# Moving eleven evictions per mixer from VectorE to ScalarE in a two-block transformer kernel

## The chip, the cores and the metric

The kernel is one program on one core of a Trainium2 chip. The metric is device time in microseconds (us) for one execution. Time is also split by engine: TensorE (PE, with its weight loads as PEld), VectorE (DVE), ScalarE (ACT), GpSimd (POOL) and the queue of SyncE (SP) that issues most transfers. TensorE's clock is granted at one of two levels, 1.2 and 2.4 GHz; a granted clock of 0.50 in a row is the lower one.

## The reference, cut to what matters

512 tokens of width 1024, fp32. A first block (sliding-window attention beside a state-space mixer, then a product-key expert layer) is followed by a second block of two layers. Each layer is a swiglu, a mixer of four parts that share one input projection, and another swiglu. The change lies in the mixers of these two layers:

```python
z = rmsnorm(x, mix_norm) @ w_in
# a: sparse attention, 4 heads of 64, the 256 best keys of an indexer
q = rmsnorm(q, g_q); k = rmsnorm(k, g_k)
logits = einsum(q, k_selected) * 64**-0.5 + bias          # softmax, times v
# b: gated linear attention, chunked
k_dec = k * exp(b_last - b);  S = exp(b_last) * S + k_dec.T @ v
# c: conv, rmsnorm, silu
# d: latent attention, 4 heads of 96
q  = (rmsnorm(c_q,  g_qa)  @ w_uq ).reshape(L, 4, 96)
kv = (rmsnorm(c_kv, g_kva) @ w_ukv).reshape(L, 4, 64 + 64)
k_nope, v = kv[..., :64], kv[..., 64:]
k = rmsnorm(concat(k_nope, k_pe), g_k)                     # then rope on 32 of the 96
y = concat([y_a, y_b, y_c, y_d]) @ w_out
```

## The kernel before, in words

Every engine's instruction stream is written out by hand. A mixer (class `Mixer`, made once for each layer) has a generator for each engine and each part: `pe_a`, `ac_a`, `ve_a` for the sparse attention, `pe_d`, `ac_d`, `ve_d` for the latent attention, `pe_b`, `ac_b`, `ve_b` for the linear attention, `*_conv` for the convolution, `ve_search` for the selection of keys. `order2` makes one list of steps, and `merged2` walks it on each engine, so the list fixes the order of each engine's queue. It begins a0 d0 c20 a1 d1 c21 a2 d2 a3 d3 a4 d4 a5 d5 a6 d6 b0 b1 a7 d7 b2 b3 a8 d8. Each engine issues in order; waits are on semaphores, and `merged2` starts on ScalarE only when every engine has ended the stage ahead of it, VectorE's last search step there being the last to end.

What the steps do, tokens in four tiles of 128:

- a0 to a3: TensorE turns (`pe_turn`, line 458) the sparse attention's queries and keys into four PSUM tiles `aT` of 128x512 (two pairs of heads, n=0 queries, n=1 keys), in banks 0 to 2. VectorE scales each by a column of gains into `qTa` (line 3419) and `kTa` (line 3421).
- d0, d1: TensorE expands the queries (line 3435), ScalarE scales them by the token's reciprocal norm (line 3478) and squares them (line 3479). d2, d3: TensorE expands keys and values (line 3442) in PSUM banks 4 to 6, and VectorE scales both halves of each of the four tiles, keys into `KD` (line 3525) and values into `VD` (line 3526).
- c21: VectorE normalizes the convolution (line 3171), ScalarE applies Silu (line 3132).
- a4: TensorE makes the first scores (lines 2687 and 2690), VectorE their maxima (lines 2761 and 2762), ScalarE their exponentials (line 2728).
- d4: ScalarE squares `KD` (line 3486); VectorE sums the squares (line 3905). d5: VectorE applies the norms (line 3914). d6, d7: VectorE does the rotary part of queries, then keys (lines 3542 to 3547).
- b0: VectorE multiplies the decayed keys (line 3680), TensorE turns them into PSUM tile `kdT` (bank 7), and VectorE copies it to `KDD` (line 3682). b1: VectorE makes a difference of decays (line 3686), ScalarE its exponential (line 3614). b2: VectorE multiplies the queries into `QX` (line 3693); TensorE's b2 and b3 wait for it (line 3570). `KDD` is read by TensorE much later, with the second block of the linear attention.

Of the kernel before, what the change touches and what calls it, by code (L numbers as in the profile page):

```python
# [13 lines left out]
ALU = mybir.AluOpType  # L14
# [708 lines left out]
class Bias:  # L723
# [23 lines left out]
    ve = po = sp = pe  # L747
# [2034 lines left out]
class Mixer:  # L2782
# [610 lines left out]
    def pe_a(self):  # L3393
        k, pe, at, l = self.k, self.k.pe, self.k.at, self.l
        for hp in range(2):
            for n, src in enumerate((self.AQ, self.AK)):
                pe.wait_ge(*at("hn", l, n))
                pe_turn(k, [src[:, i, 128 * hp:128 * hp + 128] for i in range(4)], 128, ("aT", l, hp, n), 0, 3)
                yield
        for h in range(4):  # L3400
            pe.wait_ge(*at("bt", l, h))
        yield from self.att_a.pe("aTd", l, 1, 1)

    def ac_a(self):
        k, ac, at, l = self.k, self.k.ac, self.k.at, self.l
        for _ in range(4):
            yield
        ac.wait_ge(*at("cn", l, 1))
        ac.wait_ge(*at("uqd", l, 3))
        yield from self.att_a.ac()  # L3410

    def ve_a(self):
        k, ve, v, at, l = self.k, self.k.ve, self.k.ve.e, self.k.at, self.l
        ve.wait_ge(*at("rl", l, 3, 7))
        for hp in range(2):
            for n, (g, dst) in enumerate(((f"aq{l}", self.qTa), (f"ak{l}", self.kTa))):
                ve.wait_ge(*at("aT", l, hp, n))
                if n == 0:
                    last = v.tensor_scalar(dst[:, hp, :], k.got("aT", l, hp, n), k.col(g), 0.125, ALU.mult, ALU.mult)
                else:  # L3420
                    last = v.tensor_scalar(dst[:, hp, :], k.got("aT", l, hp, n), k.col(g), None, ALU.mult)
                last.then_inc(*ve.free(("aT", l, hp, n)))
                ve.note("aTd", l, hp, n)
                yield
        yield from self.att_a.ve()

    def pe_d(self):
# [40 lines left out]
    def ac_d(self):  # L3468
        k, ac, at, l = self.k, self.k.ac, self.k.at, self.l
        a = ac.e.activation  # L3470
        for i in range(4):
            if i == 2:
                yield
            r = self.RR[:, i:i + 1]
            ac.wait_ge(*at("uqd", l, i))
            ac.wait_ge(*at("drstd", l))
            o = k.got("uq", l, i)[:, 0:384]
            a(self.QD[:, i].rearrange("p h e -> p (h e)"), o, ACT.Copy, scale=r).then_inc(*ac.up("qd", l, i))
            a(self.QSQ[:, 384 * i:384 * i + 384], o, ACT.Square, scale=r).then_inc(*ac.free(("uq", l, i)))
            ac.note("dhsq", l, i)  # L3480
        yield
        yield
        yield
        ac.wait_ge(*at("kd", l, 3))
        ac.wait_ge(*at("kdp", l))
        a(self.KSQ, self.KD.rearrange("p i h e -> p (i h e)"), ACT.Square).then_inc(*ac.up("dksq", l))
        for n in range(2):
            ac.wait_ge(*at("dhv", l, n))
            a(k.st[:, 32 + 16 * n:48 + 16 * n], k.st[:, 32 + 16 * n:48 + 16 * n],
              ACT.Sqrt).then_inc(*ac.up("dhs", l, n))  # L3490
        yield
        for _ in range(2):
            yield
        ac.wait_ge(*at("dscale", l))
        sc = k.st[:, 100:102]
        for n, dst in enumerate((self.qTd, self.kTd)):
            for h in range(4):
                ac.wait_ge(*at("dT", l, h, n))
                a(dst[0:96, h, :], k.got("dT", l, h, n)[0:96], ACT.Copy,
                  scale=sc[0:96, n:n + 1]).then_inc(*ac.free(("dT", l, h, n)))  # L3500
                ac.note("dTd", l, h, n)
                if h % 2:
                    yield

        ac.wait_ge(*at("cn", l, 1))
        yield from self.att_d.ac()

    def ve_d(self):
        k, ve, v, at, l = self.k, self.k.ve, self.k.ve.e, self.k.at, self.l
        QD, KD = self.QD, self.KD  # L3510

        sc = k.st[:, 100:102]
        v.memset(sc, 1.0).then_inc(*ve.up())
        ve.after().tensor_copy(sc[0:64, 0:1], k.col(f"dqc{l}")[0:64])
        v.tensor_copy(sc[0:64, 1:2], k.col(f"dkc{l}")[0:64]).then_inc(*ve.up())
        ve.after().tensor_scalar(sc[:, 0:1], sc[:, 0:1], 96.0 ** -0.5, None, ALU.mult).then_inc(*ve.up("dscale", l))
        yield
        yield
        for i in range(4):
            if i == 2:  # L3520
                yield
            r = self.RR[:, 4 + i:5 + i]
            ve.wait_ge(*at("ukvd", l, i))
            o = k.got("ukv", l, i).rearrange("p (h e) -> p h e", e=128)
            v.tensor_scalar(KD[:, i, :, 0:64], o[:, :, 0:64], r, None, ALU.mult)
            v.tensor_scalar(self.VD[:, i], o[:, :, 64:128], r, None, ALU.mult).then_inc(*ve.free(("ukv", l, i)))
            ve.note("kd", l, i)
        yield
        ve.wait_ge(*at("dhsq", l, 3))
        for n, (x, sq) in enumerate(((self.QSQ, ("dhsq", l, 3)), (self.KSQ, ("dksq", l)))):  # L3530
            ve_headvar(k, x.rearrange("p (i h e) -> p i h e", h=4, e=96), 4, 96, 32 + 16 * n, sq, ("dhv", l, n))
        yield
        for n, x in enumerate((QD, KD)):
            ve_headscale(k, x, 4, 96, 32 + 16 * n, ("dhs", l, n))
        yield
        R1, R2, R3, R4 = self.RT

        def rope(n, x):
            C1, S2, C2, S1 = (bc(g, 2, 4) for g in self.GT[n])
            x1, x2 = x[:, :, :, 64:80], x[:, :, :, 80:96]  # L3540
            ve.wait_ge(*at("gt", l))
            ve.after().tensor_tensor(R1, x1, C1, ALU.mult)
            v.tensor_tensor(R2, x2, S2, ALU.mult)
            v.tensor_tensor(R3, x2, C2, ALU.mult)
            v.tensor_tensor(R4, x1, S1, ALU.mult).then_inc(*ve.up())
            ve.after().tensor_tensor(x1, R1, R2, ALU.subtract)
            v.tensor_tensor(x2, R3, R4, ALU.add).then_inc(*ve.up("rope", l, n))

        rope(0, QD)
        yield  # L3550
        rope(1, KD)
        for _ in range(4):
            yield

        yield from self.att_d.ve()
# [45 lines left out]
    def ac_b(self):  # L3601
        k, ac, at, l = self.k, self.k.ac, self.k.at, self.l
        a = ac.e.activation
        CB, CS = self.CB, self.CS
        ac.wait_ge(*at("cs", l))
        for i in range(4):
            s = slice(128 * i, 128 * i + 128)
            a(self.KDT[:, s], CB[:, s], ACT.Exp, scale=-1.0, bias=CB[:, 128 * i + 127:128 * i + 128])
            last = a(self.DE[:, i:i + 1], CB[:, 128 * i + 127:128 * i + 128], ACT.Exp)
        last.then_inc(*ac.up("kde", l))  # L3610
        yield
        QES = self.ATT[0].rearrange("p h n -> p (h n)")
        ac.wait_ge(*at("qes", l))
        a(QES, QES, ACT.Exp).then_inc(*ac.up("qese", l))
        yield
        ac.wait_ge(*at("qx", l))
        a(QES, CB, ACT.Exp).then_inc(*ac.up("qe0", l))
        yield

        def block(i):  # L3620
            for n in range(10):
                if n < 8:
                    c, N = 8 * i + n, 16 * (n + 1)
                    if c >= 4:
                        ac.wait_ge(*at("ba", l, c - 4))
                    a(self.KE[c % 4][:, 0:N], CB[:, 128 * i:128 * i + N], ACT.Exp, scale=-1.0,
                      bias=CS[:, c:c + 1]).then_inc(*ac.up("kex", l, c))
                yield
            yield

        yield from block(0)
        for i in range(4):
            if i < 3:
                yield from block(i + 1)
            yield
            ac.wait_ge(*at("bo_", l, i))
            a(self.btmp[:, i], self.BV[:, i, :].rearrange("p (h e) -> p h e", e=64),
              ACT.Square).then_inc(*ac.up("bsq", l, i))
        ac.wait_ge(*at("bhv", l))
        a(k.st[:, 0:16], k.st[:, 0:16], ACT.Sqrt).then_inc(*ac.up("bhs", l))  # L3640
# [32 lines left out]
    def ve_b(self):  # L3673
# [4 lines left out]
        ve.wait_ge(*at("kde", l))  # L3678
        ve.wait_ge(*at("pj", ("bk", l)))
        v.tensor_tensor(KDT, KDT, BK, ALU.mult).then_inc(*ve.up("kdt", l))  # L3680
        ve.wait_ge(*at("kdT", l))
        v.tensor_copy(self.KDD.rearrange("p i n -> p (i n)"), k.got("kdT", l)).then_inc(*ve.free(("kdT", l)))
        ve.note("kdd", l)
        yield
        QES, QX = self.ATT[0].rearrange("p h n -> p (h n)"), self.QX
        v.tensor_tensor(QES.rearrange("p (n m) -> p n m", m=16), CB.rearrange("p (n m) -> p n m", m=16),
# [392 lines left out]
```

## Time and profile before

| | us |
|---|---|
| runs of the kernel before | 3853.77, 3854.79, 3840.77; median 3853.77 |
| profiled execution, its own time | 3855.75 |
| its span in the profile | 3854.5 |
| second stage of the first mixer, ScalarE's first instruction to the output projection | 2153.35 to 2300.84 |
| the same in the second mixer | 3294.31 to 3434.50 |

The span is what the profiled instructions cover, and the run's own time is 1.25 us longer. The two stages of the table have the same instructions; they last 147.49 and 140.19 us. A row of the timeline gives start, duration, engine, line, operation, output and inputs, and in brackets how long the engine had been idle and what ended that.

### The profile page before, as it was taken

To read this page: it belongs to the slowest core of one execution; us is meant where nothing else is said; L and a number is where in the kernel's file an instruction comes from. 1 tells how busy PE (TensorE), PEld (TensorE's weight loads), DVE (VectorE), ACT (ScalarE), POOL (GpSimd) and SP (SyncE) were. 2 spreads that over 40 slices of the span, in tenths; PEclk is the share of its full clock that TensorE was granted. 3 is DMA by queue.
4 is the path that set the end of the run, shared out by engine and by line. 5 is a ranking of instruction groups with operands and counts; after the bars stand their busy time and mean duration, and the time that the engine had idled before them with its cause. 6 is when DMAs were issued, how large, how long until landed. Compare 5 with 4: busy or idle time off the path is not lost.

```text
span 3854.5 us, 46791 instructions
## 1 busy us (share of the span) xinstructions
PE 3670.0 (95%) x18466; PEld 3098.8 (80%) x18466; DVE 2293.3 (59%) x3998; ACT 1366.0 (35%) x2368; POOL 575.0 (15%) x610
## 2 busy tenths in 40 slices
PE   9779999999999999999999689999999999689999
PEld 7767999988888888888877568888888877468887
DVE  5746899988788898433268744332433269644332
ACT  3344333444333343423243343232323243344221
POOL 8600012211445563000000100000000000100000
PEclk9779999999999999999999699999999999799999
DMA  3003388899999999233322002233223221012332
GB/s 129 12 12 93 103 276 276 269 323 331 380 375 392 388 384 360 89 94 98 104 72 60 20 23 87 95 97 104 82 94 103 88 72 55 20 50 82 99 104 72
DMA packets 275994, 574.72 MB, mean 149 GB/s; under 512 B 19952, under 2 KB 159376, under 8 KB 275648
## 3 DMA queue, kind: packets, MB, share of 16 engines
q1 hardware_dynamic: 238816, 437.42, 34.2%
q0 software_dynamic: 36864, 134.23, 9.3%
q8 instruction: 146, 2.39, 0.3%
q14 instruction: 72, 0.59, 0.0%
q10 hardware_dynamic: 96, 0.08, 0.0%
HBM read 517.92 MB, written 53.74 MB: 148 GB/s over the span
## 4 chain that ended last, share of the span: by engine, by line
PE 82%; DVE 6%; DMA 1%; ACT 1%; issue 1%; POOL 0%; DVEq 0%; SPq 0%; ACTq 0%; POOLq 0%
PE ps L358 25%; PE ps L359 24%; PE ps L360 24%; PE ps L2053 1%; PE ps L2687 1%; PE ps L590 1%; PE ps L2690 1%; PE ps L2715 1%; DVE arena L3248 1%; DVE st L3246 1%; DMA wraw<-in_ut 1%; PE ps L2697 0%; DVE arena L3149 0%; PE ps L3187 0%; PE ps L2041 0%
## 5 line engine op out<-in xcount | busy, mean ns | idle before, releaser
L349 DVE TENSOR_TENSOR wlast<-wraw,wlast 128x1024 fp32r<-128x1024 f32 x406 | 495.5, 1224 | 461.2 <-ACT wlast L339 461.1
L358 PE MATMUL ps<-XH,wlast 128*128 128x512 f32 (+2 forms) x1936 | 727.3, 376 | 18.2 <-DVE XL L637 12.5
L359 PE MATMUL ps<-XL,wlast 128*128 128x512 f32 (+2 forms) x1936 | 712.8, 368 | 0.0
L360 PE MATMUL ps<-XH,wlast 128*128 128x512 f32 (+2 forms) x1936 | 712.5, 368 | 0.0
L339 ACT ACTIVATE wlast<-wraw 128x1024 fp32r<-128x1024 f32 x406 | 426.7, 1055 | 305.4 <-PE ps L360 248.6
L349 DVE TENSOR_TENSOR wtwo<-wraw,wtwo 128x1024 fp32r<-128x1024 f32 x212 | 259.5, 1226 | 288.9 <-ACT wtwo L339 288.6
L358 PEld LDWEIGHTS ps<-XH,wlast 128*128 128x128 f32 x1936 | 368.6, 190 | 70.7 <-issue 19.8
L359 PEld LDWEIGHTS ps<-XL,wlast 128*128 128x128 f32 x1936 | 369.3, 191 | 44.5
L360 PEld LDWEIGHTS ps<-XH,wlast 128*128 128x128 f32 x1936 | 368.5, 190 | 45.3
L358 PE MATMUL ps<-XH,wtwo 128*128 128x512 f32 (+1 forms) x968 | 367.0, 379 | 2.4 <-DVE XL L637 2.4
L359 PE MATMUL ps<-XL,wtwo 128*128 128x512 f32 (+1 forms) x968 | 360.3, 372 | 0.0
L360 PE MATMUL ps<-XH,wtwo 128*128 128x512 f32 (+1 forms) x968 | 359.8, 372 | 0.0
L339 ACT ACTIVATE wtwo<-wraw 128x1024 fp32r<-128x1024 f32 x212 | 223.6, 1055 | 210.3 <-PE ps L360 163.0
L2138 POOL DMA_INDIRECT arena<-in_v,arena x128 | 237.7, 1857 | 191.8 <-DVE X L2262 86.5
L2138 POOL DMA_INDIRECT arena<-in_u,arena x128 | 148.1, 1157 | 587.6 <-DVE arena L2239 433.0
L3212 POOL TENSOR_SCALAR_AFFINE_SELECT arena<-arena 128x128 f32<-128x128 f32 x6 | 3.5, 576 | 1497.9 <-DVE arena L3232 1497.9
L358 PEld LDWEIGHTS ps<-XH,wtwo 128*128 128x128 f32 x968 | 184.9, 191 | 27.3 <-issue 2.6
L359 PEld LDWEIGHTS ps<-XL,wtwo 128*128 128x128 f32 x968 | 185.4, 192 | 24.4
L360 PEld LDWEIGHTS ps<-XH,wtwo 128*128 128x128 f32 x968 | 185.0, 191 | 24.7
L358 PE MATMUL ps<-wlast,AH 128*128 128x512 f32 x504 | 196.1, 389 | 0.0
L359 PE MATMUL ps<-wlast,AH 128*128 128x512 f32 x504 | 196.1, 389 | 0.0
L360 PE MATMUL ps<-wlast,AL 128*128 128x512 f32 x504 | 196.1, 389 | 0.0
(500 smaller groups left out, 6614.6 us busy)
## 6 DMA issues: line engine op xcount, KB each, us to landing
wraw<-in_ut SPq DMA_DIRECT2D x128, 512.0 KB, 5.2
wraw<-in_v SPq DMA_DIRECT2D x128, 512.0 KB, 7.1
wraw<-in_ffn_gate SPq DMA_DIRECT2D x88, 512.0 KB, 3.5
wraw<-in_ffn_up SPq DMA_DIRECT2D x88, 512.0 KB, 3.5
wraw<-in_ffn_down SPq DMA_DIRECT2D x88, 512.0 KB, 3.5
wraw<-in_w_in SPq DMA_DIRECT2D x58, 512.0 KB, 3.8
acts<-arena SPq DMA_DIRECT2D x128, 192.0 KB, 5.6
gates<-arena SPq DMA_DIRECT2D x12, 2048.0 KB, 12.7
```

The lines of the kernel that those rows point to most:

```text
L339: ac.e.activation(W.items[n][7], W.rawof(n), ACT.Copy).then_inc(*ac.up("whi", n))
L349: ve.e.tensor_tensor(W.items[n][8], W.rawof(n), W.items[n][7], ALU.subtract).then_inc(*ve.up("wlo", n))
L358: mm(out, lh, rh, start=start, stop=False)
L359: mm(out, lh, rl, start=False, stop=False)
L360: return mm(out, ll, rh, start=False, stop=stop)
L590: pe.e.matmul(o[:, c:c + 128], k.X[:, i, j * 128:(j + 1) * 128], self.D[i], start=True, stop=True).then_inc(*pe.up("xT", n, i, "column", j))
L2053: last = pe.e.matmul(self.gate_bank[:, 128 * (t % 4):128 * (t % 4) + 128], self.O[n % self.AHEAD][:, 0, t // 2, :, t % 2], self.RH[n % sel ...
L2138: g.indirect_dma_start(out=self.RB[n % self.ROWS], out_offset=None, in_=tables[n // PICKS], in_offset=bass.IndirectOffsetOnAxis(ap=self.PL ...
L2687: pe.e.matmul(o[:, 0:nk], self.qf(2 * hp + h, i), self.kf(2 * hp + h, nk), start=True, stop=False)
L2690: last = pe.e.matmul(o[:, lo:nk], one, x, start=False, stop=x is adds[-1][1])
L2715: last = pe.e.matmul(o[:, 64 * h:64 * h + 64], self.PT[h][:, 128 * kb:128 * kb + 128], self.V4[:, kb, 2 * hp + h, :], start=kb == 0, stop= ...
L3246: ve.after().max(m8, src).then_inc(*ve.up())
```

## The change

In each of the two mixers, ScalarE takes over three kinds of work from VectorE: the two scaled copies of turned keys (`kTa`), the eight scaled copies of the expanded keys and values (`KD`, `VD`), and the copy of the turned decayed keys (`KDD`). They become ACTIVATE instructions with function Copy; the first ten have a column as scale. On ScalarE the `kTa` copies stand in steps a1 and a3, the `KD` and `VD` copies in d2 and d3, and the `KDD` copy in b1, ahead of the exponential of line 3614. TensorE waits for one more event ahead of the first scores, since `qTa` and `kTa` now come from two engines.

```diff
@@ pe_a
+        pe.wait_ge(*at("aTd", l, 1, 0))
         yield from self.att_a.pe("aTd", l, 1, 1)
@@ ac_a
-        for _ in range(4):
+        ac.wait_ge(*at("sc", l, 3, 7))
+        for hp in range(2):
+            yield
+            ac.wait_ge(*at("aT", l, hp, 1))
+            ac.e.activation(self.kTa[:, hp, :], k.got("aT", l, hp, 1), ACT.Copy,
+                            scale=k.col(f"ak{l}")).then_inc(*ac.free(("aT", l, hp, 1)))
+            ac.note("aTd", l, hp, 1)
             yield
@@ ve_a
-            for n, (g, dst) in enumerate(((f"aq{l}", self.qTa), (f"ak{l}", self.kTa))):
...
+            ve.wait_ge(*at("aT", l, hp, 0))
+            v.tensor_scalar(self.qTa[:, hp, :], k.got("aT", l, hp, 0), k.col(f"aq{l}"), 0.125, ALU.mult,
+                            ALU.mult).then_inc(*ve.free(("aT", l, hp, 0)))
+            ve.note("aTd", l, hp, 0)
+            yield
+            yield
@@ ac_d (and the same loop, with tensor_scalar, taken out of ve_d)
+        for i in range(4):
+            if i == 2:
+                yield
+            r = self.RR[:, 4 + i:5 + i]
+            ac.wait_ge(*at("ukvd", l, i))
+            o = k.got("ukv", l, i).rearrange("p (h e) -> p h e", e=128)
+            a(self.KD[:, i, :, 0:64], o[:, :, 0:64], ACT.Copy, scale=r)
+            a(self.VD[:, i], o[:, :, 64:128], ACT.Copy, scale=r).then_inc(*ac.free(("ukv", l, i)))
+            ac.note("kd", l, i)
@@ ac_b, ahead of the wait for "qes"
+        ac.wait_ge(*at("kdT", l))
+        a(self.KDD.rearrange("p i n -> p (i n)"), k.got("kdT", l), ACT.Copy).then_inc(*ac.free(("kdT", l)))
+        ac.note("kdd", l)
@@ ve_b
-        ve.wait_ge(*at("kdT", l))
-        v.tensor_copy(self.KDD.rearrange("p i n -> p (i n)"), k.got("kdT", l)).then_inc(*ve.free(("kdT", l)))
-        ve.note("kdd", l)
```

## Rows read from the trace of the kernel before

**Rows 1.** The page: span, busy time, share and instructions of each engine

```profile
span 3854.5 us, 46791 instructions
PE 3670.0 (95%) x18466; PEld 3098.8 (80%) x18466; DVE 2293.3 (59%) x3998; ACT 1366.0 (35%) x2368; POOL 575.0 (15%) x610
```

**Rows 2.** Chain that ended last, first mixer: start, us, engine, output, line

```profile
2163.22 0.54 ACT arena L2728 x3
2163.76 1.38 ACT arena L3486
2165.16 1.76 DVE st L3905
...
2174.88 1.13 PE ps L458 x4
...
2179.57 0.59 DVE wlent L3693
```

**Rows 3.** Timeline of ScalarE, first mixer

```profile
2153.35 0.58 ACT L3478 ACTIVATE wlent<-ps,st 128x384 f32<-128x384 f32 x1 [16.33 <-DVE arena L3248]
...
2156.61 0.62 ACT L3479 ACTIVATE arena<-ps,st 128x384 f32<-128x384 f32 x1
2157.25 1.28 ACT L3132 ACT_TABLE_LOAD   x1
...
2159.71 1.28 ACT L2728 ACT_TABLE_LOAD   x1
2162.95 0.37 ACT L2728 ACTIVATE arena<-ps,st 128x128 f32<-128x128 f32 x1 [1.96 <-DVE st L2762]
...
2178.05 1.25 ACT L3499 ACTIVATE arena<-ps,st 96x512 f32<-96x512 f32 x2
```

**Rows 4.** Timeline of TensorE and VectorE, first mixer

```profile
2157.42 0.48 DVE L3525 TENSOR_SCALAR wlent<-ps,st 128x256 f32<-128x256 f32 x1
...
2158.51 1.88 PE L3442 MATMUL ps<-arena 128*128 128x512 f32 x4
...
2159.07 0.74 DVE L3421 TENSOR_SCALAR arena<-ps,cols 128x512 f32<-128x512 f32 x1
...
2160.33 0.48 PE L2687 MATMUL ps<-arena 64*128 64x128 f32 x2
...
2162.29 0.42 DVE L2761 TENSOR_REDUCE st<-ps 128x2 f32<-128x256 f32 x1 [0.91 <-PE ps L2690]
...
2174.14 0.68 DVE L3680 TENSOR_TENSOR wlent<-wlent,arena 128x512 f32<-128x512 f32 x1
...
2176.03 0.69 DVE L3682 COPY wlent<-ps 128x512 f32<-128x512 f32 x1 [1.21 <-PE ps L458]
2176.64 0.68 DVE L3686 TENSOR_TENSOR wlent<-arena 128x512 f32<-128x512 f32 x1
...
2179.49 2.77 DVE L3693 TENSOR_TENSOR wlent<-wlent,arena 32x512 f32<-32x512 f32 x4
```

**Rows 5.** Timeline of ScalarE, second mixer

```profile
3296.88 0.58 ACT L3478 ACTIVATE wlent<-ps,st 128x384 f32<-128x384 f32 x1 [0.58 <-PE ps L3435]
...
3299.39 1.28 ACT L3132 ACT_TABLE_LOAD   x1
...
3305.15 0.37 ACT L2728 ACTIVATE arena<-ps,st 128x128 f32<-128x128 f32 x1 [2.02 <-DVE st L2762]
```

**Rows 6.** ScalarE's groups by form, 2000 to 2330 us: busy us, mean ns

```profile
L2998 ACT ACTIVATE arena<-ps 128x256 f32<-128x256 f32 x20 | 7.2, 383 | 32.6 <-PE ps L360 32.6
...
L2737 ACT ACTIVATE arena<-ps 128x512 f32<-128x512 f32 x8 | 4.8, 595 | 9.0 <-PE ps L2697 8.7
...
L2728 ACT ACTIVATE arena<-ps,st 128x256 f32<-128x256 f32 x8 | 3.7, 476 | 0.0
```

**Rows 7.** Stretches from first wait on `QX` to output projection, both mixers

```profile
2182.30:2300.80 118.50, 104.20 (x524) 75.32 (x524) 49.25 (x117) 49.02 (x146) 12.03 (x32) 0.82 0.00 1
...
3324.50:3434.40 109.90, 93.59 (x524) 68.77 (x524) 48.94 (x116) 48.50 (x146) 10.88 (x32) 0.90 0.00 1
```

More of the change, by code:

```diff
@@ L3415, in ve_a @@
         for hp in range(2):
-            for n, (g, dst) in enumerate(((f"aq{l}", self.qTa), (f"ak{l}", self.kTa))):
[L3417 to L3424, printed above, removed]
+            ve.wait_ge(*at("aT", l, hp, 0))
[4 more added lines that the diff above has]
+            yield
         yield from self.att_a.ve()
@@ L3481, in ac_d @@
         yield
-        yield
+        for i in range(4):
[7 more added lines that the diff above has]
+            ac.note("kd", l, i)
         yield
@@ L3516, in ve_d @@
         ve.after().tensor_scalar(sc[:, 0:1], sc[:, 0:1], 96.0 ** -0.5, None, ALU.mult).then_inc(*ve.up("dscale", l))
[L3517 to L3528, printed above, removed]
+        for _ in range(4):
+            yield
         ve.wait_ge(*at("dhsq", l, 3))
```

## The prediction

> **What bounds the kernel now.** I read the page first: TensorE is busy for 95% of the span, VectorE for 59%, ScalarE for 35% [rows 1]. VectorE's load as such sets nothing; it counts only where TensorE waits for it. So I went to the chain that ended last, and in it to the two stretches that the change touches, one in each mixer. There the chain leaves TensorE. In the first mixer it runs over ScalarE's first exponentials and the square of the keys (1.38 us), VectorE's sum of squares, the norms and rotary part on VectorE, the turning of the decayed keys on TensorE, and on to the product `QX` on VectorE [rows 2]. The timeline of each engine then tells which of them is late at each step. ScalarE stands idle for 1.96 us ahead of the first exponential, with its table already loaded [rows 3]. VectorE stands idle for 0.91 us ahead of the first maxima and 1.21 us ahead of the copy of `kdT` [rows 4]. These three gaps are what the change can use up or give back.
>
> **What leaves VectorE.** Per mixer two instructions like that of line 3421 (0.74 us), eight of 128x256 (0.48 us) and one copy (0.69 us) [rows 4]: 1.5 + 3.8 + 0.7 = 6.0 us of durations, 12 us over both. Ten of the eleven stand ahead of the first maxima, and VectorE already waits there for TensorE, so their absence only makes that wait longer. What counts is when ScalarE has done them.
>
> **ScalarE's queue ahead of the first exponential, first mixer.** It starts at 2153.35, when the stage ahead ends; that doesn't move. The eight query instructions start 0.466 us apart ((2156.61 - 2153.35)/7), though each takes 0.58 us: neighbours overlap by 0.116 us [rows 3]. The scaled key tile is a 128x512 from PSUM with a column as scale; the nearest row is line 3499 with 96x512, two in 1.25 us of 0.68 us each, so 0.57 us from start to start [rows 3]. The first one stands between query pairs, and its tile has been turned by then: the Silu table load moves from 2157.25 to 2157.82. Load and Silu keep their 2.46 us (2157.25 to 2159.71), and the first of the new key and value instructions starts at 2160.28, where the exponential's table load stood before.
>
> A scaled 128x256 from PSUM isn't in the trace in this use. With a column as operand it takes 476 ns, without one 383 ns [rows 6]; less the overlap of 0.116 that is 0.36 from start to start. The bounds are 0.27 (the 383 ns row less the overlap) and 0.60 (rows of 128x384 without any overlap). I take 0.36, the row with the same shape and operand. Four of them bring `kTa`'s second tile to 2161.72, done at 2162.40. Four more start from 2162.29 and end at 2163.85, and the table load (1.28 us) ends at 2165.14. Two things are thus late:
>
> - TensorE's first scores, at 2160.33 before, wait for that tile: 2162.5. From their start to the first exponential it was 2162.95 - 2160.33 = 2.62 us [rows 3, 4], so by this path 2165.12.
> - ScalarE itself, ready at 2165.14.
>
> Both give the same: the exponentials start 2.2 us later. The square of the keys and the sum behind it follow them rigidly [rows 2], and so does all of VectorE up to line 3680: +2.2 us. The last key projection, which needs the bank of the first (free 0.8 us after 2160.28, so about 2161.1), takes half of the 1.88 us of two [rows 4] and ends by 2162.1: ahead of its use at about 2163, it costs nothing.
>
> The Trainium skill, in "ScalarE: Activation LUTs", section "What ACT_TABLE_LOAD costs", says that a switch of set costs the load of 1283 ns and a drain of about 1380 ns on top. The trace has 1.28 us for the load, and the queue goes on within 0.02 us [rows 3]; by the page's sum each mixer would lose 1.38 us more, as a load that was hidden now stands on the path. The measurement decides. The same section gives 280 ns + 0.833 ns per element with a pointer operand and 93 ns of overlap: an estimate of 400 ns from start to start, which would add 8 x 0.04 = 0.3 us per mixer.
>
> **Second mixer.** ScalarE waits 0.58 us for the third query tile [rows 5], and the first key tile (0.57 us) goes into that wait. The Silu load stays at 3299.39, the key and value instructions start at 3301.85, the second `kTa` ends at 3303.97, the last value at 3305.42, the table load at 3306.71; by the scores 3304.07 + 2.62 = 3306.69. The exponentials were at 3305.15 [rows 5]: +1.56 us.
>
> **What comes back at `kdT`.** Before, VectorE went from the start of line 3680 (2174.14) to that of line 3686 (2176.64) in 2.50 us, with the wait for TensorE and the copy between them. Now line 3686 follows directly, 0.61 us behind as after the copy [rows 4]: -1.89 us. What is next to be late is ScalarE's exponential, behind its new copy. The turned tile is done 1.86 us after the start of line 3680 (2174.88 + 1.12); copy 0.60 [rows 6], exponential about the same, 0.63, with no overlap counted: ready at about +3.1 us. `QX` needs it at 0.61 + 2.85 (2176.64 to 2179.49, line 3686 and the rotary part) = +3.46. The cover holds with some 0.35 us to spare. If it failed wholly the gain would be zero; more than 1.89 isn't there. `KDD` itself is read much later.
>
> **The sum.** First mixer +2.2 - 1.89 = +0.3; second +1.56 - 1.89 = -0.3; together 0.0 us on the profiled execution's 3855.75 (span 3854.5 and 1.25 around it). That execution is 2.0 us above the median of the runs shown, 3853.77, and I carry the difference over: forecast 3854. With the dear end of the 128x256 price each mixer loses 8 x 0.24 = 1.9 more, with the cheap end it wins back some 0.4, and without the gain at `kdT` it loses 1.9: together from -1 to +8 us. TensorE's extra wait is for an event of 2157, and ScalarE's wait for the indexer for one from the stage before: nothing. No transfer is moved.
>
> **Rivals.** A measurement of this kernel tells 0.5%, 19 us, from no change. All but one of the cases below are smaller.
>
> 1. *The clock turns against it* (slower). From `QX` to the output projection the two mixers run the same instructions in 118.5 us at a granted clock of 0.82 and 109.9 us at 0.90 [rows 7]: 8.6 us between two outcomes of the same work. The change makes TensorE idle before the first scores, in a stretch where it had worked without a gap, and moves all later work. If the second mixer gets what the first had, +8.6; with the clock already low under the first scores up to 2 us more, as these take at most twice their 1.96 us; with half of the dear bounds +12. Time 3858 to 3866. The point that decides: the granted clock in the second mixer after `QX`, and whether it is 0.5 under the first scores. For it: the new gap. Against: before, the clock fell anyway soon after the first scores. The skill ("TensorE: Matmul & The Clock Gate", "Why this matters for your kernels") says that idle gaps between bursts bring the array back to its lower rate, which speaks against this change; by it this case would hold.
> 2. *The clock turns for it* (faster): the first mixer gets what the second had, -8.6: 3845. The same rows speak for it; one of the runs before, at 3840.77, shows that 13 us lie in this kernel's own spread.
> 3. *VectorE was the bound* and gives back its 12 us: 3842. Its waits of 0.91 and 1.21 us ahead of the very places [rows 4] speak against it.
> 4. *ScalarE's queue pays more* without help of the clock: dear price and no gain at `kdT`: +8, 3862.
>
> **Chances.** Forecast (3850 to 3857) 0.50; rival 1 0.17; rival 2 0.17; rival 3 0.04; rival 4 0.10; something unseen 0.02. Eight times in ten the time should be in 3841 to 3863. For over 0.5% faster (under 3834.5) rivals 2 and 3 would have to add up: 0.04. Over 0.5% slower (above 3873) needs rivals 1 and 4 together: 0.05. Within: 0.91.
>
> **What would show it.** In the profile after: the 128x256 instructions of ScalarE 0.36 us apart; no idle time of ScalarE ahead of the first exponential but a table load that ends there; the first scores 2.2 us later than before against ScalarE's first instruction of the stage; VectorE idle for some 7 us ahead of the first maxima; line 3686 directly behind line 3680; `QX` not waiting for the exponential; its start 0.3 us later (first mixer) and 0.3 us earlier (second). Wrong would be: a wait of `QX` for ScalarE, a first exponential that is late by 4 us or more, or a stage after `QX` that changes at equal clock.

## The result, and the profile after

The changed kernel takes 3858.94 us (median of 19 runs, 3850.46 to 3863.64) against 3852.74 for the kernel before (19 runs, 3840.09 to 3859.33). The ratio is 1.0017 with a 95% interval of 1.0009 to 1.0025: 6 us slower, inside the 0.5% that was called no change, above the forecast of 3854 and its 3850 to 3857, and inside the prediction's wider 3841 to 3863. The ratios here aren't quotients of the two medians; with spreads of 13 to 37 us the two differ by up to 0.15%. Of all runs below, one of the changed kernel with fill took 9740 us and is left out of every mean. The span of the changed kernel's profiled execution is 3857.1 us. One view answers the first question at once, ScalarE's timeline in the first mixer [rows 3]:

```profile
2152.12 0.58 ACT L3482 ACTIVATE wlent<-ps,st 128x384 f32<-128x384 f32 x1 [16.69 <-DVE arena L3248]
...
2156.08 0.58 ACT L3482 ACTIVATE wlent<-ps,st 128x384 f32<-128x384 f32 x1 [0.34 <-PE ps L3439]
...
2159.50 0.46 ACT L3492 ACTIVATE wlent<-ps,st 128x256 f32<-128x256 f32 x1
2159.86 0.46 ACT L3493 ACTIVATE arena<-ps,st 128x256 f32<-128x256 f32 x1
...
2160.93 0.70 ACT L3411 ACTIVATE arena<-ps,cols 128x512 f32<-128x512 f32 x1
...
2162.56 0.52 ACT L3493 ACTIVATE arena<-ps,st 128x256 f32<-128x256 f32 x1
2163.10 1.28 ACT L2728 ACT_TABLE_LOAD   x1
2164.48 0.37 ACT L2728 ACTIVATE arena<-ps,st 128x128 f32<-128x128 f32 x1
...
2177.56 0.60 ACT L3616 ACTIVATE wlent<-ps 128x512 f32<-128x512 f32 x1 [5.54 <-PE ps L458]
2178.05 0.62 ACT L3619 ACTIVATE wlent<-wlent 128x512 f32<-128x512 f32 x1
```

The moved instructions stand in the queue without a gap, 0.36 us apart, up to the table load, and the first exponential comes 0.10 us behind the load's end. TensorE and VectorE in the same mixer [rows 4] (line 3446 is the key projection, 3685 and 3688 are the former 3680 and 3686, 3695 makes `QX`):

```profile
2160.37 1.12 PE L3446 MATMUL ps<-arena 128*128 128x512 f32 x2 [0.88 <-ACT arena L3493]
2161.88 0.46 PE L2687 MATMUL ps<-arena 64*128 64x128 f32 x2 [0.38 <-ACT arena L3411]
2163.81 0.42 DVE L2761 TENSOR_REDUCE st<-ps 128x2 f32<-128x256 f32 x1 [6.54 <-PE ps L2690]
2175.66 0.69 DVE L3685 TENSOR_TENSOR wlent<-wlent,arena 128x512 f32<-128x512 f32 x1
2176.27 0.68 DVE L3688 TENSOR_TENSOR wlent<-arena 128x512 f32<-128x512 f32 x1
2179.13 2.77 DVE L3695 TENSOR_TENSOR wlent<-wlent,arena 32x512 f32<-32x512 f32 x4
```

VectorE now waits 6.54 us for the first scores, and at `kdT` it doesn't wait at all. The second mixer's ScalarE [rows 5] and the stretches from `QX` to the output projection in both mixers [rows 7]. A row of a stretch gives its start, end and length, the busy time and instructions of PE, PEld, DVE, ACT and POOL, the granted clock, and two figures of the DMA:

```profile
3292.11 0.58 ACT L3482 ACTIVATE wlent<-ps,st 128x384 f32<-128x384 f32 x1 [16.68 <-DVE arena L3248]
...
3304.50 0.37 ACT L2728 ACTIVATE arena<-ps,st 128x128 f32<-128x128 f32 x1
```

```profile
2179.13:2298.48 119.35, 100.69 (x526) 73.18 (x525) 52.06 (x122) 49.83 (x148) 10.90 (x32) 0.83 0.00 1
3319.15:3438.39 119.24, 100.65 (x527) 73.21 (x525) 51.90 (x122) 49.67 (x148) 10.91 (x32) 0.83 0.00 1
```

All times from here on count from ScalarE's first instruction of the mixer's second stage. From the two profiles:

| us | exponential | `QX` | `QX` to projection | whole stage |
|---|---|---|---|---|
| before, mixer 1 / 2 | 9.60 / 10.84 | 26.14 / 27.39 | 121.35 / 112.80 | 147.49 / 140.19 |
| changed, mixer 1 / 2 | 12.36 / 12.39 | 27.01 / 27.04 | 119.35 / 119.24 | 146.36 / 146.28 |

What the change touches lies ahead of `QX`, and there it adds 0.87 us in one mixer and takes 0.35 in the other. Behind `QX`, in instructions that the change doesn't touch, the second mixer takes 6.4 us more and the first 2.0 less; the two spans are only 2.6 us apart, so the 6 us between the medians can't be read from these two executions alone. In the first mixer of before the clock was low from 48 to 72 us and also, longer than in the other three, from 10 to 41 (there 13 to 33). The windows 43.5 to 57.5 and 57.5 to 71 us of the second mixer show where. Before:

```profile
3337.80:3351.80 14.00, 11.06 (x38) 7.91 (x39) 5.17 (x15) 4.86 (x22) 1.47 (x5) 0.51 0.00 0
3351.80:3365.30 13.50, 13.42 (x69) 9.05 (x69) 4.45 (x12) 5.04 (x20) 1.57 (x4) 1.00 0.01 2
```

Changed:

```profile
3335.60:3349.60 14.00, 11.29 (x39) 8.14 (x39) 4.95 (x15) 5.08 (x23) 1.48 (x5) 0.51 0.00 0
3349.60:3363.10 13.50, 13.50 (x39) 8.54 (x38) 2.43 (x6) 2.43 (x10) 1.57 (x4) 0.50 0.01 2
```

The first window holds the same work in both. In the second TensorE is busy throughout in both, but gets through 69 matmuls at a granted clock of 1.00 before, and 39 at 0.50 in the changed kernel. One row of each shows the step, eight matmul records of line 2715 that start 57.35 us (before) and 57.12 us (changed) into the stage:

```profile
3351.66 1.10 PE L2715 MATMUL ps<-arena 128*128 128x64 f32 x8
```

```profile
3349.23 1.97 PE L2715 MATMUL ps<-arena 128*128 128x64 f32 x8
```

### The profile page after: what moved, and what is told of

The parts are those of the page before. It is cut to its first block, busy times and chain, and to the rows that moved or that the text cites. A ratio compares the mean times of both kernels' runs of the same rounds, so it can differ in the third digit from the quotient of the medians.

```text
span 3857.1 us, 46793 instructions
## 1 busy us (share of the span) xinstructions
PE 3677.0 (95%) x18466; PEld 3103.1 (80%) x18466; DVE 2283.1 (59%) x3976; ACT 1374.7 (36%) x2390; POOL 558.5 (14%) x610
## 4 chain that ended last, share of the span: by engine, by line
PE 82%; DVE 5%; ACT 1%; DMA 1%; issue 1%; POOL 0%; DVEq 0%; SPq 0%; ACTq 0%; POOLq 0%
PE ps L358 25%; PE ps L359 24%; PE ps L360 24%; PE ps L2053 1%; PE ps L2687 1%; PE ps L590 1%; PE ps L2690 1%; PE ps L2715 1%; DVE arena L3248 1%; DVE st L3246 1%; DMA wraw<-in_ut 1%; PE ps L3187 1%; PE ps L2697 0%; PE ps L2041 0%; PE ps L458 0%
## 5 line engine op out<-in xcount | busy, mean ns | idle before, releaser
L2138 POOL DMA_INDIRECT arena<-in_v,arena x128 | 223.6, 1747 | 208.1 <-DVE X L2262 106.4
L2589 ACT ACTIVATE HH<-arena 128x512 fp32r<-128x512 f32 x88 | 55.6, 632 | 395.8 <-DVE arena L2607 395.8
L358 PE MATMUL ps<-wlast,AH 128*128 128x512 f32 x504 | 196.1, 389 | 0.0
```

The costliest lines, as they stand in the source:

```text
L358: mm(out, lh, rh, start=start, stop=False)
L2138: g.indirect_dma_start(out=self.RB[n % self.ROWS], out_offset=None, in_=tables[n // PICKS], in_offset=bass.IndirectOffsetOnAxis(ap=self.PL ...
L2589: a(self.HH[:, f, :], s, ACT.Copy).then_inc(*ac.up("hh", *id, f))
```

## The experiments

Theory 1: the path up to `QX` is as the prediction worked it out, its sum is zero, and the 6 us are TensorE's clock. Against it stood that ScalarE's added work costs the 6 us by itself, and that one part of the change costs and the other is worth nothing. All runs below were timed on three chips, on each beside 35 runs of the kernel before (medians 3849.09, 3850.70 and 3851.15).

**One part of the change at a time.** The first moves the `KDD` copy alone:

```diff
+        ac.wait_ge(*at("kdT", l))
+        a(self.KDD..., k.got("kdT", l), ACT.Copy).then_inc(*ac.free(("kdT", l)))     # ac_b
-        v.tensor_copy(self.KDD..., k.got("kdT", l)).then_inc(*ve.free(("kdT", l)))   # ve_b
```

> Only the copy to KDD moves to ScalarE; the key tiles and the expanded keys and values stay on VectorE. Theory 1 (the chain up to QX is as worked out, the rest of the difference is TensorE's granted clock behind QX): QX starts 1.9 us earlier after ScalarE's first instruction of the stage than in the kernel before, in both mixers (about 24.3 and 25.5 us against 26.1 and 27.4), so -3.8 us at equal clock; the time comes out 3849 if the clock behaves as before, up to 9 us either side if it doesn't, and the difference is seen in the stretches with a granted clock of 0.50 behind QX. Rival 2 (the ScalarE copy at kdT costs by itself, as the other part's gain and loss cancel): QX not earlier, time 3856 or more.

3850.39 us, ratio 0.999 (0.9974 to 1.0006). `QX` starts at 24.25 and 25.41 us: 1.89 and 1.98 us earlier. VectorE's and ScalarE's timelines in its first mixer (line 3683 is the former 3680):

```profile
2180.15 0.68 DVE L3683 TENSOR_TENSOR wlent<-wlent,arena 128x512 f32<-128x512 f32 x1
2180.76 0.68 DVE L3686 TENSOR_TENSOR wlent<-arena 128x512 f32<-128x512 f32 x1
...
2183.61 2.77 DVE L3693 TENSOR_TENSOR wlent<-wlent,arena 32x512 f32<-32x512 f32 x4
```

```profile
2182.05 0.60 ACT L3614 ACTIVATE wlent<-ps 128x512 f32<-128x512 f32 x1 [5.53 <-PE ps L458]
2182.54 0.62 ACT L3617 ACTIVATE wlent<-wlent 128x512 f32<-128x512 f32 x1
```

The exponential ends at 2183.16 and `QX` needs it at 2183.61: 0.45 us of cover, where 0.35 had been worked out. The total alone wouldn't show the gain. The second is the changed kernel with the `KDD` copy put back on VectorE, the diff above turned round.

> All of the change but the copy to KDD, which stays on VectorE. Theory 1: the first exponential is late by 2.2 to 2.8 us in the first mixer and 1.6 in the second as in the changed kernel, and nothing comes back at kdT: +4 us at equal clock, 3857, more or less by what the clock does. Rival 2 (these ten instructions are the whole of the measured +6 us, the copy at kdT being worth nothing): 3859, the same as the changed kernel within 1 us. If theory 1 is right and the clock unchanged from the changed kernel, it is 3.8 us above the changed kernel: 3863.

3860.91 us, ratio 1.0017 (1.0001 to 1.0033). The exponential is at 12.29 and 12.42 us and `QX` at 28.84 and 28.96: the ten instructions cost 2.7 and 1.6 us and nothing comes back. The time alone can't tell the theory's 3863 from the rival's 3859; the start of `QX`, 1.8 and 1.9 us behind that of the changed kernel, does. The 2.7 of the first mixer has a part of its own: there the clock fell under the first scores, a pair of line 2690 took 0.79 us instead of 0.49, and ScalarE waited for the maxima:

```profile
2163.11 0.37 ACT L2728 ACTIVATE arena<-ps,st 128x128 f32<-128x128 f32 x1 [0.58 <-DVE st L2762]
```

Without that the exponential is at 11.8 us, as further below. So both parts have about the size worked out for them, and they nearly cancel.

**At equal clock.** Each run's record has its mean granted clock. Over the 105 runs of the kernel before on the three chips, the time falls by 26.6 us for each 0.01 of that clock, with a scatter of 2.4 us about the line. Set against this line:

| kernel | runs | mean clock | mean us | off the line of before, us |
|---|---|---|---|---|
| before | 105 | 0.9602 | 3851.3 | 0 |
| changed | 19 | 0.9575 | 3858.0 | -0.5 (standard error 0.5) |
| changed, once more | 12 | 0.9577 | 3858.3 | +0.4 (0.5) |
| `KDD` copy only | 12 | 0.9598 | 3848.3 | -3.9 (0.9) |
| without the `KDD` copy | 12 | 0.9581 | 3859.4 | +2.6 (0.7) |

The changed kernel lies on the line; what differs is the clock it gets. The `KDD` copy is off it by the 3.8 us worked out; the other ten instructions, worked out at 3.8 to 4, by 2.6. The 35 runs of before on each chip lie 0.5 us below the line on two chips and 1.1 above it on the third, which the standard errors leave out. The line may mix cause and effect, as what lengthens a run can also change its mean clock, so the proof has to come from holding the clock.

> The changed kernel as it is, once more beside the kernel before on one chip. Theory 1 (the difference is a matter of the clock's outcomes, which are many in both kernels): at the mean granted clock that it gets, its time is that of the kernel before at the same clock, within 1 us; on average 3 to 8 us slower. If the first result was chance: no difference. A look at its mixers should show low stretches behind the search of 24 us or more in most, 10 to 14 in some.

This was the repeat: 3860.80 us, ratio 1.0017 (0.9999 to 1.0035). Both its mixers kept the low clock to 71 us, as both of the changed kernel's first profile did: four mixers of four. All four had waited 4.4 us for the latent attention's first exponentials, the clock fell at 43.5 to 43.75 us, and stayed low for some 27. In the second mixer of before the wait and the fall are the same and the clock was low for 13.5 us; in its first the wait was 1.91 us, the fall at 48 and the low stretch 24 us. With the `KDD` copy only it was 10 and 14 us, without it 27 and 10. Two or four mixers of each kernel are few; the mean clocks of the table carry the argument.

**Holding the clock.** A helper puts matmuls whose result nobody reads where TensorE waits:

```diff
+    def fill(self, n, tag):
+        o = k.open(3, 4, "fill", self.l, tag)
...
+        for _ in range(n):
+            k.pe.e.matmul(o, k.ident[:, :], k.CM[:, :], start=True, stop=True)
@@ Attention.pe, ahead of scores(1)
+            if n == 0 and self.fill:
+                self.fill(1 if id[0] == "a" else 4, id[0])
@@ pe_b, ahead of the waits for "kdt" and "qx"
+        self.fill(6, "k")
+        self.fill(3, "q")
```

> The kernel before, with idle stretches of TensorE in the mixers filled by matmuls of 128x512 whose result nobody reads: 1 ahead of the second scores of the sparse attention, 6 ahead of the wait for the decayed keys, 3 ahead of the wait for QX, 4 ahead of the second scores of the latent attention. At the full clock they take 0.86 us each and fit in the gaps (9, 4 and 4 us). Theory 1 (the low clock behind QX is what the mixers pay with): the granted clock stays at 1.00 through both mixers, the stretch from QX to the output projection falls to 100 to 106 us in both (from 118.5 and 109.9), the time to 3830 to 3838. Rival 2 (the clock is not what costs there, VectorE and ScalarE bound the stretch): no change or slower, 3853 to 3860.

> The changed kernel with the same 14 filling matmuls in each mixer. Theory 1: with the clock held up in both, only the chain's own sum is left, so it comes out equal to the kernel before with fill, within 1.5 us (the first mixer +0.3 to +0.9, the second -0.3). Rival 2 (the change costs 6 us by the work on ScalarE): 6 us above the kernel before with fill. If the clock falls in one of them all the same, its stretches with a granted clock of 0.50 account for the difference, half of their busy length.

Kernel before with fill: 3844.48 us, 0.9983 (0.9962 to 1.0003). Changed kernel with fill: 3840.01 us, 0.9972 (0.9955 to 0.9989). The first misses its size, 3830 to 3838: the low clock came back for 3 to 7 us in each place where a wait was left over. (`QX` is at 27.04 us in the first mixer before, with 26.14 without fill, but not by the fill: the clock was low until 2.75 us there, the exponential came at 10.87 for 9.60, and from it to `QX` it took 16.17 us for 16.54.) The second asked for equal within 1.5 us and got a changed kernel that is 4.5 below, not 6 above; the intervals don't tell it from equal. The sharper test fills a single place, the wait that ends at about 46 us (4.4 us, or 1.91 in the first mixer of before), in each kernel: the fill counts are 0 but for 5 ahead of the latent attention's second scores.

> The kernel before with five filling matmuls (128x512, result unread) in one place of each mixer: TensorE's wait of 4.4 us for the first exponentials of the latent attention, some 42 to 46 us behind ScalarE's first instruction of the stage. Theory 1 (what differs between the two kernels is how long the clock stays at the lower level behind this wait: 14 us in one mixer of the kernel before, 24 in the other, 27.5 in both of the changed kernel): the clock doesn't fall there, and the time drops by 5 to 12 us per mixer, to 3832 to 3842. Rival 2 (the wait doesn't matter): 3849 to 3855 as the kernel before.

> The changed kernel with the same five filling matmuls in the same place. Theory 1: the same time as the kernel before with them, within 2 us, as the long low stretch that cost the changed kernel its 6 us is gone in both. Rival 2 (ScalarE's added work costs the 6 us): still 6 us above the kernel before with the five, whatever the fill brings. Rival 3 (the clock's loss lies in the new gap of TensorE ahead of the first scores): also still some us above.

3845.30 us, 0.9985 (0.997 to 1.0001), and 3844.20 us, 0.9984 (0.9968 to 1.0000). The two medians are 1.1 us apart. Windows 43.5 to 57.5 and 57.5 to 71 of the second mixer, kernel before with the five, then changed kernel with them:

```profile
3322.90:3336.90 14.00, 13.75 (x69) 8.87 (x67) 6.16 (x18) 6.37 (x28) 2.60 (x8) 1.00 0.01 1
3336.90:3350.40 13.50, 12.19 (x61) 7.98 (x61) 4.85 (x12) 3.82 (x14) 0.46 (x1) 1.00 0.00 1
```

```profile
3318.30:3332.30 14.00, 13.76 (x69) 8.84 (x67) 6.10 (x18) 6.37 (x28) 2.59 (x8) 1.00 0.01 2
3332.30:3345.80 13.50, 12.19 (x62) 8.02 (x61) 4.85 (x12) 3.82 (x14) 0.46 (x1) 1.00 0.00 0
```

The clock doesn't fall, the rows are alike, and the 6 us are gone from the medians, with all of ScalarE's added work in place. How firm is that? The means are 3842.5 and 3843.6 us, the changed kernel 1.1 above with a standard error of 2.8, which by itself hardly excludes 6. With 14 matmuls it is 4.7 below, with 3.7. Both pairs together give -1.0 with 2.2, and 6 us are three standard errors away. So rival 2, ScalarE's added work, is excluded, though not by the sharper pair alone. Rival 3, a loss in TensorE's new gap ahead of the first scores, goes the same way, since that gap is untouched in both pairs. The size was missed again, 3845 for at most 3842, and for the kernel before the interval just includes no gain: its one profile, with 136.3 and 136.2 us for the mixers, from 140 to 147, promised more than the median shows. Why the other executions give less isn't shown.

**Why the low stretch is long so often in the changed kernel.** It has `QX` at 27.04, the kernel before at 26.14 or 27.39. A memset or two on VectorE move that place:

```diff
@@ ve_b, ahead of the wait for "qese"
+        ve.wait_ge(*at("uqd", l, 3))
+        ve.wait_ge(*at("ukvd", l, 3))
+        v.memset(BMK, 0.0).then_inc(*ve.up())      # the second kernel: v.memset(SB, 0.0) ahead of it
```

> The changed kernel with one memset of 128x256 more on VectorE (0.27 us) ahead of QX in each mixer, which puts QX at about 27.3 us behind ScalarE's first instruction, where the second mixer of the kernel before has it (27.39). Theory 1a (the length of the low stretch behind the search is decided by where TensorE's work lies to a fraction of a microsecond): the low stretch ends in some executions at 57 us and in others at 71, as in the kernel before, so the time falls by 3 to 6 us to 3852 to 3855 although 0.5 us of work was added. Theory 1b (something else than that place decides it): 3858 to 3860.

> The same with two memsets (0.54 us), QX at about 27.6 us. Theory 1a: again another share of long and short low stretches, time anywhere from 3848 to 3861, at equal granted clock 1.1 us above the changed kernel. Theory 1b: 3859 to 3861, all low stretches long.

3855.88 us, 1.0020 (1.0005 to 1.0035), and 3854.70 us, 1.0009 (0.9992 to 1.0027). The first lies between the two theories' ranges, and its mean, 3858.5 us, is that of the changed kernel. The low stretch ends at 57 in one mixer and at 71 in the other with one memset, and at 72 and 57.5 with two. Short stretches do come back with more work added, but the mixer with `QX` at 27.31 had the long one and the one at 27.24 the short one, and the intervals overlap that of the changed kernel. So the place isn't shown to decide.

**A version that beats both.** The `KDD` copy alone, with fill in six places (12 matmuls ahead of the convolution's row sums, 1, 8, 2, 6, and 4 ahead of `pe_out`'s turns), then with a larger fill (14, 1, 10, 4, 6, 4), the latter also for the kernel before.

> Only the copy to KDD on ScalarE, and filling matmuls in all large waits of TensorE in the mixer: 12 ahead of the convolution's row sums, 1 ahead of the second scores, 8 ahead of the wait for the decayed keys, 2 ahead of QX, 6 ahead of the second scores of the latent attention, 4 ahead of the output projection's turns. Theory 1: the gain of 3.8 us at equal clock comes on top of a clock that stays up: each mixer 130 to 134 us from ScalarE's first instruction to the output projection, the time 3826 to 3834, below every other version, and with a smaller spread. Rival 2: no better than the changed kernel with fill, 3840.

> The kernel before with filling matmuls in all large waits of TensorE in the mixers (14 ahead of the convolution's row sums, 1, 10, 4, 6, and 4 ahead of the output projection's turns). With the clock up in both mixers it should be 3836 to 3842; beside the next kernel it gives the worth of the KDD copy with the clock held.

> The KDD copy on ScalarE with the same fill. The chain's working: 3.8 us under the kernel before with this fill (1.9 in each mixer, seen in the start of QX), 3832 to 3837. If the copy is worth nothing once the clock is held: the same as it. If the larger fill spills over into the work that follows, both come out slower than the version with the smaller fill, 3836.

3835.59 us, 0.9957 (0.9939 to 0.9975); kernel before with the larger fill 3837.68, 0.9966 (0.9952 to 0.9981); `KDD` copy with it 3832.93, 0.9949 (0.9931 to 0.9966), the lowest median of all: 0.5% or some 18 us below the kernel before. The first missed its 3826 to 3834, its mixers took 136.1 and 136.0 us for 130 to 134, with the clock low from 27.5 to 37.75 us in both, and its spread is no smaller (3822.65 to 3848.78); the other two came out in their ranges. The two medians with the larger fill are 4.7 us apart, and their intervals overlap, so the worth of the copy is read from `QX`. `QX` moves from 25.67 and 25.62 to 24.20 and 24.18, 1.5 us in each mixer and not 1.9: at the full clock TensorE's turns, which VectorE no longer waits for, take 0.66 us and not 1.12. That is 2.9 of the 4.7. Whole stages of the last kernel:

```profile
2154.57:2292.91 138.34, 126.70 (x629) 85.14 (x629) 73.94 (x166) 65.51 (x181) 18.66 (x49) 0.93 0.03 10
3288.94:3420.80 131.86, 119.20 (x628) 79.06 (x629) 73.73 (x166) 65.34 (x181) 18.64 (x49) 1.00 0.03 11
```

The same instructions last 131.86 us at a clock of 1.00 and 138.34 at 0.93. In the first of these mixers the clock was low from 113 to 130 us, which this fill doesn't reach.

## Why the prediction was right or wrong, point by point

- **Prices on ScalarE:** right. 128x256 with a column: 0.46 to 0.52 us, 0.36 from start to start, as taken; the key tile 0.70 and 0.57. By its formula for an operand from a column, the Trainium skill ("ScalarE: Activation LUTs", "What ACT_TABLE_LOAD costs") gives an estimate of 0.40; the row decides.
- **No drain at the table load:** right. Load 1.28 us, the exponential 0.10 us behind it, on the path now. The 1.38 us of drain in the same section don't appear here.
- **First exponential:** second mixer +1.55, worked out +1.56. First mixer +2.76 for +2.2. The term that was mis-sized is the query expansion on TensorE, taken as it was in that mixer before: there the clock was full from 0.25 us on, in the changed kernel's profile only from 2.5, and ScalarE waited 0.34 us for the fourth query tile, as it did in the second mixer (0.37). Where the clock had risen early (first mixer of the changed kernel with fill, and with the single fill) the exponential is at 11.81: +2.21.
- **Gain at `kdT`:** right in size and cover (1.89 and 1.98 us alone, 0.45 us to spare).
- **Sum up to `QX`:** +0.87 and -0.35, worked out +0.3 and -0.3; the first by the term above. With the clock risen early, the changed kernel with the single fill, which stands behind `QX`, has it at 26.46: +0.32.
- **VectorE's 12 us (the prediction's rival 3):** nothing came of them. In each mixer 5.6 us became waiting ahead of the maxima, 6.54 for 0.91.
- **The clock unchanged:** this step failed. The sum put the clock at nothing, and the 0.0 us that it forecast is what the changed kernel shows at equal clock (-0.5, standard error 0.5); its lower clock is worth the 6 us. What came is rival 1, given 0.17, with its mechanism behind `QX` and some 6 us of its 8.6. By the time alone it could be rival 4 (3862) too, whose dear price and missing gain the rows exclude. That 3858.94 lies within 3841 to 3863 is no merit of the sum, as that range took in both outcomes of the clock. The sign could not be read from the one profile of before, which held one long and one short low stretch. Rival 1's guess at the cause, the new gap ahead of the first scores, isn't borne out: the scores ran at full clock in the changed kernel (0.46 us for the first pair, 0.48 before), and with that gap left in, a fill elsewhere removed the difference. In one mixer, that without the `KDD` copy, the clock did fall under them, and cost 0.5 us.

What stays open: why the changed kernel gets the lower clock more often, as it seems in the stretch behind the wait that ends at 46 us. TensorE's instructions from 46 to 57 us are the same in the second mixers of both kernels, 0.23 us earlier in the changed one, and the clock rises behind them in one and not in the other.

## What to carry to other kernels

When work moves to an idle engine, look for the wait that ends last at its new place: here ten moved instructions cost 1.6 to 2.8 us per mixer because ScalarE's first exponential and TensorE's first scores, for which the others wait, stand behind them, while one copy taken out of a wait gave 1.9. Price such a change at equal granted clock, by the clock of every run and not by two profiles, before explaining a difference of a few us. And a wait of TensorE of 4 us can cost more behind it than in it (13.5 us at half the clock are 6.75 us lost); in the changed kernel a few unread matmuls there gave back more than the change had cost.

## What the runs showed of the hardware

- The granted clock that follows a wait has few outcomes and large steps: after the same wait of 4.4 us, from 43.5 or 43.75 us on, it was low for 13.5 us in three mixers (before, and one each of the two kernels with memsets) and for some 27 in five (four of the changed kernel, one with a memset), with the same dense work behind, 6 to 7 us apart in time. Other waits there, of 1.9 to 5.9 us, had 10 to 14 us or 24 to 27 behind them. The Trainium skill ("TensorE: Matmul & The Clock Gate", "Why this matters for your kernels") has idle gaps bring the lower rate and busy work the higher; the fall in or behind the waits agrees, and so does its absence once the wait is filled. That dense work can run 27 us at the lower level, as here, no run explains.
- Five unread matmuls of 128x512 took 4.51 us in that wait; over two mixers the medians on that chip fell by 5.4 us in the kernel before (its interval just includes none) and by 16.6 in the changed one (3860.80 to 3844.20).
- ScalarE's 128x256 from PSUM with a column as scale starts every 0.36 us; on VectorE four of them took 1.65 us (2157.42 to 2159.07 [rows 4]), 0.41 each. The move was no loss in price, only in order; the key tile too starts the next one after 0.57 us on ScalarE and after 0.66 on VectorE (2159.07 to 2159.73).
